# Latent attention: scores of a head as three products of high and low parts, with the queries scaled before they are transposed

## The reference, cut to what matters

```python
q = (rmsnorm(c_q, q_norm_g) @ w_q_up).reshape(B, S, N_HEADS, QK_DIM)
kv = (rmsnorm(c_kv, kv_norm_g) @ w_kv_up).reshape(B, S, N_HEADS, 2 * HEAD_DIM)
k = jnp.concatenate([k_nope, jnp.broadcast_to(k_rope[:, :, None, :], ...)], axis=-1)
q = rmsnorm(q, q_head_g)
k = rmsnorm(k, k_head_g)
q = jnp.concatenate([q[..., :HEAD_DIM], rope(q[..., HEAD_DIM:], positions)], axis=-1)
...
logits = jnp.einsum('bhqd,bhkd->bhqk', qi, k) * scale     # blocks of 128 queries
w = jax.nn.softmax(jnp.where(mask, logits, -jnp.inf), axis=-1)
o = jnp.einsum('bhqk,bhkd->bhqd', w, v)
o = o * jax.nn.silu(gate)
```

## Time and profile before

| | before |
|---|---|
| median of 3 runs | 1319.96 us |
| the profiled execution | 1320.29 us |
| its span in the trace | 1318.1 us |
| TensorE busy | 1297.5 us (98%) |
| VectorE busy | 762.6 us (58%) |
| ScalarE busy | 639.9 us (49%) |
| GpSimd busy | 344.7 us (26%) |
| mean granted TensorE clock | 0.999 |

### The profile page before, as it was taken

The page is one execution under the profiler, slowest core; times in us unless marked ns, Lnnn a source line. Parts: engine busy times, 40 slices in busy tenths (PEclk is TensorE's granted clock), DMA queues, the critical chain, the costliest instruction groups (busy, mean ns, idle before and its releaser), DMA issues.

```text
span 1318.1 us, 17841 instructions
## 1 busy us (share of the span) xinstructions
PE 1297.5 (98%) x6478; PEld 1086.4 (82%) x6478; DVE 762.6 (58%) x1205; ACT 639.9 (49%) x1159; POOL 344.7 (26%) x393
## 2 busy tenths in 40 slices
PE   7999999999999999999999999999999999999998
PEld 6997878778888888888888878888888888888986
DVE  5656999835652235898444642335466335578843
ACT  5379778624532325998244422514244234355632
POOL 2228877400000007773000000000000000668620
PEclk9999999999999999999999999999999999999999
DMA  5332100122222232001322333332232321421121
GB/s 186 85 112 65 45 25 14 49 95 97 96 96 96 96 96 81 17 0 32 108 99 85 93 95 96 96 96 64 85 100 92 126 99 55 129 64 49 34 64 64
DMA packets 70595, 104.66 MB, mean 79 GB/s; under 512 B 3460, under 2 KB 30840, under 8 KB 70392
## 3 DMA queue, kind: packets, MB, share of 16 engines
q1 hardware_dynamic: 69312, 99.44, 24.0%
q0 software_dynamic: 1088, 4.17, 1.1%
q10 hardware_dynamic: 120, 0.05, 0.0%
HBM read 101.55 MB, written 2.10 MB: 79 GB/s over the span
## 4 chain that ended last, share of the span: by engine, by line
PE 90%; DVE 5%; ACT 2%; issue 2%; DMA 0%; DVEq 0%; POOL 0%; SPq 0%; ACTq 0%; POOLq 0%
PE ps L491 24%; PE ps L493 24%; PE ps L492 24%; PE ps L688 2%; PE ps L991 2%; PE ps L846 2%; PE ps L701 1%; PE ps L935 1%; PE ps L836 1%; PE ps L715 1%; PE ps L667 1%; PE ps L837 1%; DVE sp L2052 1%; PE ps L716 1%; DVE sp_l L2057 1%
## 5 line engine op out<-in xcount | busy, mean ns | idle before, releaser
L1655 DVE TENSOR_TENSOR w_lo<-stage,w_hi 128x1024 fp32r<-128x1024 f32 (+4 forms) x189 | 225.1, 1191 | 421.7 <-ACT w_hi L1087 421.6
L1087 ACT ACTIVATE w_hi<-stage 128x1024 fp32r<-128x1024 f32 (+4 forms) x189 | 192.0, 1016 | 463.2 <-PE ps L493 462.0
L491 PE MATMUL ps<-a0h,w_hi 128*128 128x512 f32 x512 | 204.6, 400 | 0.8 <-DVE q_lo L2232 0.8
L493 PE MATMUL ps<-a0h,w_lo 128*128 128x512 f32 x512 | 200.0, 391 | 0.0
L492 PE MATMUL ps<-a0l,w_hi 128*128 128x512 f32 x512 | 199.5, 390 | 0.0
L2336 POOL TENSOR_TENSOR small<-small 128x16 f32<-128x16 f32 (+2 forms) x14 | 32.4, 2317 | 391.1 <-DVE small L1733 285.9
L491 PE MATMUL ps<-w_hi,a0h 128*128 128x512 f32 (+1 forms) x320 | 122.3, 382 | 0.1
L493 PE MATMUL ps<-w_hi,a0l 128*128 128x512 f32 (+1 forms) x320 | 119.9, 375 | 0.0
L492 PE MATMUL ps<-w_lo,a0h 128*128 128x512 f32 (+1 forms) x320 | 119.8, 374 | 0.0
L493 PEld LDWEIGHTS ps<-a0h,w_lo 128*128 128x128 f32 x512 | 96.1, 188 | 20.6
L491 PEld LDWEIGHTS ps<-a0h,w_hi 128*128 128x128 f32 x512 | 96.2, 188 | 20.1 <-issue 1.3
(11 more groups left out here) (324 smaller groups left out, 2841.9 us busy)
## 6 DMA issues: line engine op xcount, KB each, us to landing
stage<-in_a_w_in SPq DMA_DIRECT2D x48, 512.0 KB, 3.8
stage<-in_ple_w_gate SPq DMA_DIRECT2D x16, 512.0 KB, 3.3
stage<-in_w_kv_shared SPq DMA_DIRECT2D x16, 512.0 KB, 3.6
stage<-in_sb_w_in SPq DMA_DIRECT2D x16, 512.0 KB, 3.7
stage<-in_a_w_out SPq DMA_DIRECT2D x16, 512.0 KB, 3.3
stage<-in_b_w_in SPq DMA_DIRECT2D x16, 512.0 KB, 3.7
stage<-in_mla_w_in SPq DMA_DIRECT2D x8, 512.0 KB, 3.9
stage<-in_sb_w_out SPq DMA_DIRECT2D x8, 512.0 KB, 3.3
```

The lines of the kernel that those rows point to most:

```text
L491: pe.matmul(bank, wh, mh, start=start and not seeded, stop=False, skip_group_check=seeded)
L493: return pe.matmul(bank, wl, mh, start=False, stop=stop, skip_group_check=seeded)
L1087: act.activation(slab(w_hi[r % 2], L, nk, w), slab(stage[r % 4], L, nk, w), ACT.Copy).then_inc(S("hi_ready"), 1)
L1655: dve.tensor_tensor(slab(w_lo[r % 2], L, nk, w), slab(stage[r % 4], L, nk, w), slab(w_hi[r % 2], L, nk, w), ALU.subtract)\
```

## The change

Scores are computed from high and low parts of queries and keys, in three fp32r products instead of one in float32. For that the queries must be scaled before they are transposed, which GpSimd does with a multiplication over all 96 columns in place of the copy of 64; the gain of the queries is negated, so the scores come out negative, the mask has the other sign, and the row minimum is at once the bias of the exponential. `qT_h`, `qT_l`, `kT_h` and `kT_l` have one buffer each. ScalarE reads the high part out of bank 6, and VectorE, after it, the low part (`head_lo`); `qT_ok` and `kT_ok` are now set by VectorE. Of the four blocks of probabilities VectorE scales the two long ones, ScalarE the two short ones. TensorE runs three steps of the gate tile between the transposes of queries and of keys, and one behind them.

Apart from the attention: the first load comes in two halves; the wait in `out0` is moved behind three more steps; the negated sink of the window attention is gone, and some semaphores of the last norm have other names.

```diff
-        "causal": np.where(i[None, :] <= i[:, None], 0.0, BIG),
+        "causal": np.where(i[None, :] <= i[:, None], 0.0, -BIG),
...
-    qT = [put(f"qT{s}", [P, T], 10 + 2 * s) for s in range(2)]
-    kT = [put(f"kT{s}", [P, T], 14 + 2 * s) for s in range(2)]
+    qT_h, qT_l = (put(f"qT_{n}", [P, T], kb, F32R) for n, kb in (("h", 10), ("l", 12)))
+    kT_h, kT_l = (put(f"kT_{n}", [P, T], kb, F32R) for n, kb in (("h", 14), ("l", 16)))
...
+            if r == 0:
+                sp_.dma_start(stage[0][:, 0:nk, 0:w // 2], src[:, :, 0:w // 2]).then_inc(S("first_in"), 16)
+                sp_.dma_start(stage[0][:, 0:nk, w // 2:w], src[:, :, w // 2:w]).then_inc(loaded[0], 16)
+                return
...
-                if k % 2 == 0:
+                if r == 0 and k == 0:
+                    pe.wait_ge(S("first_lo"), 1)
+                elif k % 2 == 0:
...
                     if L.name == "out0" and k == 0 and n == 3:
+                        continue
+                    if L.name == "out0" and k == 1 and n == 3:
                         pe.wait_ge(S("src_ready"), source(first_item["x0"]))
+                        products(0, n)
+                    if L.name == "proj0" and g == k == 0 and n == 2:
+                        pe.wait_ge(S("lo_ready"), 1)
                     if L.name == "q_up" and g == k == 0 and n == 3:
...
-                pe.matmul(ps[b][:, c:c + n], qT[s][0:QK, j * P:(j + 1) * P], kT[s][0:QK, 0:n],
-                          start=j != 0, stop=False, skip_group_check=True)
+                to, rows = ps[b][:, c:c + n], slice(j * P, (j + 1) * P)
+                pe.matmul(to, qT_h[0:QK, rows], kT_h[0:QK, 0:n], start=j != 0, stop=False, skip_group_check=True)
+                pe.matmul(to, qT_h[0:QK, rows], kT_l[0:QK, 0:n], start=False, stop=False, skip_group_check=True)
+                pe.matmul(to, qT_l[0:QK, rows], kT_h[0:QK, 0:n], start=False, stop=False, skip_group_check=True)
                 pe.matmul(ps[b][:, c + j * P:c + n], ident_r[:, :], causal_r[:, :], start=False, stop=True, skip_group_check=True)\
                     .then_inc(S("s_done"), 1)
...
-                pe.wait_ge(S("p_ready"), MB * h + (n + 1))
+                if n < 2:
+                    pe.wait_ge(S("p_ready"), 2 * h + n + 1)
+                else:
+                    pe.wait_ge(S("p_act"), 2 * h + n - 1)
...
-                mla_gate_tile(lin["mla_gate1"], i, 7, 4 * s, 4 * s + 2)
+                mla_gate_tile(lin["mla_gate1"], i, 7, 4 * s, 4 * s + 3)
...
-                out_rows(0, 4 * s, 4 * s + 2, (0,), s == 1)
+                out_rows(0, 4 * s, 4 * s + 3 - s, (0,), s == 1)
...
-                mla_gate_tile(lin["mla_gate1"], i, 7, 4 * s + 2, 4 * s + 4)
+                mla_gate_tile(lin["mla_gate1"], i, 7, 4 * s + 3, 4 * s + 4)
...
-                out_rows(0, 2, 4, (0,), False)
+                out_rows(0, 3, 4, (0,), False)
...
-        def head_T(h, s, sem, to, g, ok, bank=6):
+        def head_hi(h, sem, to, g, bank=6):
+
+
             act.wait_ge(S(sem), h + 1)
-            if not (isinstance(h, int) and h < 2):
-                act.wait_ge(S("s_done"), MB * (h - 1))
-            act.activation(to[s][0:QK, :], ps[bank][0:QK, :], ACT.Identity, scale=gain(g, 0, QK)).then_inc(S(ok), 1)
+            if h:
+                act.wait_ge(S("s_done"), MB * h)
+            act.activation(to[0:QK, :], ps[bank][0:QK, :], ACT.Identity, scale=gain(g, 0, QK)).then_inc(S("qk_hi"), 1)
...
-                               scale=scale, accum_out=ssum[:, j:j + 1]).then_inc(S("exp_done"), 1)
+                               scale=-1.0, accum_out=ssum[:, j:j + 1]).then_inc(S("exp_done"), 1)
...
-            probs(h, s, (lambda: head_T(h + 1, 1 - s, "qT_done", qT, "q", "qT_ok")) if more else None)
+            probs(h, s, (lambda: head_hi(h + 1, "qT_done", qT_h, "q")) if more else None)
             if more:
-                head_T(h + 1, 1 - s, "kT_done", kT, "k", "kT_ok")
+                head_hi(h + 1, "kT_done", kT_h, "k")
+            act.wait_ge(S("rsum_ok"), h + 1)
+            for j in (1, 0):
+                at = slice(QRY_COL[j], QRY_COL[j] + (j + 1) * P)
+                act.activation(pr[:, at], pr[:, at], ACT.Identity, scale=rsum[:, j:j + 1]).then_inc(S("p_act"), 1)
...
-        dve.wait_ge(S("q_ss_ok"), 4)
-
-        def maxima(h):
-            def scaled(j, n):
-                link.wait(n)
-                scale = q_ss[:, h, j:j + 1] if isinstance(h, int) else q_ss[:, bass.ds(h, 1), j]
-                dve.scalar_tensor_tensor(nb[:, j:j + 1], mx[:, j:j + 1], -1.0, scale, ALU.mult, ALU.mult).then_inc(S("nb_done"), 1)
-
-            last = None
+        def minima(h):
+
+
             for r, j in enumerate(reversed(range(MB))):
                 b, c = QRY_BANK[j]
                 dve.wait_ge(S("s_done"), MB * h + (r + 1 if j > 1 else MB))
-                n = link.mark(dve.tensor_reduce(mx[:, j:j + 1], ps[b][:, c:c + (j + 1) * P], AX.X, ALU.max))
-                if last:
-                    scaled(*last)
-                last = (j, n)
-                if r == 0:
-                    scaled(*last)
-                    last = None
-            scaled(*last)
+                dve.tensor_reduce(nb[:, j:j + 1], ps[b][:, c:c + (j + 1) * P], AX.X, ALU.min).then_inc(S("nb_done"), 1)
 
         def normalize(h):
             dve.wait_ge(S("exp_done"), MB * h + MB)
-            link(dve.reciprocal(rsum, ssum))
-            for j in reversed(range(MB)):
+            if h:
+                dve.wait_ge(S("p_act"), 2 * h)
+            dve.reciprocal(rsum, ssum).then_inc(S("rsum_ok"), 1)
+            dve.wait_ge(S("rsum_ok"), h + 1)
+            for j in (3, 2):
                 at = slice(QRY_COL[j], QRY_COL[j] + (j + 1) * P)
                 dve.tensor_scalar(pr[:, at], pr[:, at], rsum[:, j:j + 1], None, ALU.mult).then_inc(S("p_ready"), 1)
 
-        def probs_T(h):
+        def head_lo(n, high, low, g, ok, bank=6):
+
+            dve.wait_ge(S("qk_hi"), n)
+            dve.scalar_tensor_tensor(low[0:QK, :], ps[bank][0:QK, :], gain(g, 0, QK), high[0:QK, :], ALU.mult, ALU.subtract)\
+               .then_inc(S(ok), 1)
+
+        def probs_T(h, between=None):
             if h:
                 dve.wait_ge(S("o_done"), h)
             for b, (c, n) in enumerate(((0, T), (T, 384), (896, 384))):
+                if b == 1 and between:
+                    between()
                 dve.wait_ge(S("pT_a"), 3 * h + (b + 1))
                 dve.tensor_tensor(prT_l[:, c:c + n], ps[3 + b][:, 0:n], prT_h[:, c:c + n], ALU.subtract).then_inc(S("pT_b"), 1)
...
         def mla_step(h):
             i, s = h // 2, h % 2
-            maxima(h)
+            minima(h)
+            more = h < HEADS - 1
+
+            def q_low():
+                head_lo(2 * h + 3, qT_h, qT_l, "q", "qT_ok")
+
             if h:
-                probs_T(h - 1)
+                probs_T(h - 1, q_low if more else None)
+            else:
+                q_low()
             if h == 1:
                 split_to(lin["mla_gate1"].load0 + 1)
             normalize(h)
+            if more:
+                head_lo(2 * h + 4, kT_h, kT_l, "k", "kT_ok")
             if h == 0:
                 head_sums(k_ss, 4 * HD, "k")(lin["kv_up"], G, MB - 1, None)
...
                 mla_sum(h - 1)
 
+        head_lo(1, qT_h, qT_l, "q", "qT_ok", 0)
+        head_lo(2, kT_h, kT_l, "k", "kT_ok", 1)
         for h in range(HEADS):
...
-            dve.scalar_tensor_tensor(nb_w[s], mx_w[s], -1.0, neg_sink[:, h:h + 1].to_broadcast([P, MB]), ALU.mult, ALU.min).then_inc(S("wnb_done"), 1)
+            dve.tensor_scalar(nb_w[s], mx_w[s], sink[:, h:h + 1], -1.0, ALU.max, ALU.mult).then_inc(S("wnb_done"), 1)
...
-            pool.tensor_copy(q_ring[s][:, :, 0:HD], q[:, :, 0:HD])
-            rotate(q_ring[s][:, :, HD:QK], q[:, :, HD:QK], 0, s, "qk_ring")
+            scale = q_ss[:, h, :].rearrange("p (m o) -> p m o", o=1)
+            link(pool.tensor_tensor(q_ring[s][:, :, :], q, scale.to_broadcast([P, MB, QK]), ALU.mult))
+            turned = q_ring[s][:, :, HD:QK]
+            pool.tensor_tensor(rope_b[s][:, :, 0:16], turned[:, :, 16:32], rope[:, 1, :, 0:16], ALU.mult)
+            link(pool.tensor_tensor(rope_b[s][:, :, 16:32], turned[:, :, 0:16], rope[:, 1, :, 16:32], ALU.mult))
+            link(pool.tensor_tensor(turned, turned, rope[:, 0, :, :], ALU.mult))
+            pool.tensor_tensor(turned, turned, rope_b[s][:, :, :], ALU.add).then_inc(S("qk_ring"), 1)
```

More of the change, by code:

```diff
@@ L291, in build @@
     q_ss, k_ss = little(HEADS, MB), little(HEADS, MB)
-    mx, nb, ssum, rsum, esink = little(MB), little(MB), little(MB), little(MB), little(MB)
-    nb_w, ssum_w, es_w = ([little(MB) for _ in range(2)] for _ in range(3))
-    neg_sink = little(HEADS)
+    nb, ssum, rsum, esink = little(MB), little(MB), little(MB), little(MB)
+    nb_w, ssum_w = ([little(MB) for _ in range(2)] for _ in range(2))
+    both_w = [little(MB, 2) for _ in range(2)]
     mx_w = [little(MB) for _ in range(2)]
@@ L616, in do @@
```

(34 more changed lines are left out.)

14 lines of the change are left out of this document (6 added, 8 removed).

## The result

The changed kernel takes 1345.88 us (median of 4 runs, 1343.03 to 1346.32) against 1319.86 for the kernel before, run beside it: a ratio of 1.019 (95% interval 1.0177 to 1.0202), or +26.0 us. The forecast was 1335.0 with a range of 1325 to 1342. The direction was right; the size was not, and the time lies outside the range.

A forecast was written before the change was run, and what follows sets the result against it. TensorE, busy 98% of the span, was taken to bound the kernel. Terms of 14.4 (heads 2 to 14), +1.8 (edges), -1.1 (`out0`) and -0.1 (start) gave +15.0, so 1335.0 us, range 1325 to 1342.

The forecast's parts named there:

- The mechanism: Latent attention: values wait for VectorE's low part of the keys, about 0.7 us in even heads, near 1.9 in odd.
- New scores: Each latent attention head: three products take 2.34 us instead of 2.56, a gain of 0.22.
- lower bound of 2.13: New scores' time in us if a product needs only its columns' share without change of weights.
- four rivals: Short scalings 1328 (0.18), faster 1315 (0.10), whole GpSimd operations 1341 (0.10), scores not cheaper 1338.5 (0.05).
- whole exclusions: Rival, odd heads: each scaling waits for a whole GpSimd operation, loss 2.8 per head, +21.4 in all, 1341; chance 0.10.
- the edges of the attention: First scores +1.5, head 0 -0.4, head 1 +1.6, last head -0.9: together +1.8 us, taken as ±1.5.
- Head 0: First latent attention head: no values, TensorE's work 7.2 us against 7.61 before, so -0.4.
- Head 1: Second latent attention head: weight split and head 0's sums delay VectorE, values 1.0 later than other heads' 0.57: +1.6 us.
- The terms per head: Heads 2 to 14: seven even at 0.57 us and six odd at 1.73, 14.4 together.
- The start: First products could begin earlier, but transposes wait for the input's loads: -0.1 us, bounds ±0.4.
- `out0`: TensorE's wait of 1.15 us there is covered by nine products: -1.1, bounds 0 and -1.15.
- the last head: Last latent attention head: values' wait of 1.57 us for VectorE falls without the negating steps, -0.9.

The follow-up runs named there:

- Float32 scores: Changed kernel with float32 scores, bank 6 read once, double buffers and gate products 6 and 6: 1315.87 us, ratio 0.9966 to the kernel before.
- the small edits alone: Kernel before with only first weights in halves, delayed out0 product, and window attention's and last norm's small changes: 1318.23 us against 1320.54, ratio 0.9984.
- zero products: Changed kernel with zero-tile products in TensorE's waits, 7 before head 0's scores, 4 or 8 behind key transposes: 1340.59 us, ratio 1.0155 to the kernel before.
- a change of order on VectorE alone: Changed kernel with the key's low part ahead of the two scalings in every head: 1332.76 us, ratio 1.0098 to the kernel before.
- its pause: Kernel before with two throw-away VectorE readings that TensorE waits for ahead of head 0's scores: 1322.32 us, ratio 1.0014.
- Behind 2.9 us: Kernel before with four throw-away VectorE readings ahead of head 0's scores instead of two: 1325.56 us, ratio 1.0044.

## Why the prediction was wrong

**The mechanism was right.** The values wait for the key's low part in 14 heads (the forecast's 15 counts one too many, since head 0 has no values and the last head no keys), by about 1.1 in even and 2.2 in odd ones, for a forecast 0.7 and 1.9. Float32 scores take all of that away, and the run is then below the one with the small edits alone: scaling on GpSimd, the minima and ScalarE's two scalings cost nothing in the heads. No run has three products without the second reading, so the two were not priced apart. New scores took 2.39 (194.27 to 196.66) for a forecast 2.34; its lower bound of 2.13 is not worked out there, and nothing hung on it. None of the four rivals came as a time; what is true of the one for whole exclusions stands below.

**The step that failed: the clock, which the sum put at nothing, in the edges of the attention first.** Head 0 was put at -0.4 because "TensorE's work is 7.2". That counts its work at full clock, right behind the new wait of 1.5 that the same paragraph puts in front of it. The clock fell there, and head 0 took 10.23. The zero products brought it to 7.10, so the work was as forecast, and 3.1 of the 10.23 were clock. The same omission costs 1.0 in head 1 (3.37 from the values to the next scores, 2.34 in other heads), 0.5 in head 2 and 1.5 in head 5. That is 6.1 by the rows; the zero products gave back 5.3, as they also put off head 0's scores by 0.5. It is half of the 11.0 between forecast and result. No term of the sum and no bound had a clock in it. With the clock full the changed kernel takes 1340.59, 5.6 above the forecast and inside the range; the omitted clock is what puts it outside.

**Head 1** was put at +1.6 and lost 4.1. Its values started 9.81 after the scores, not 8.0. 1.0 of the 4.1 is clock. The rest is VectorE's queue: the sum of head 0's keys and the first minima made the query's low part late, the key transposes waited 0.98 for it, and then came a weight split of 1.21, which the forecast did name.

**The terms per head** were right in kind and small in size. Even heads: 9.63 - 8.81 = 0.82 each for a forecast 0.57. The chain is longer than its readings: the low part takes 0.74, not 0.68, and 0.28 pass from its end to the first product of the values (191.65 to 191.93) where I had allowed 0.03 to 0.05. Head 1's key transposes did start 0.05 behind the low part that they waited for:

```profile
133.94 0.74 DVE L1955 SCALAR_TENSOR_TENSOR qT_l<-ps,gains,qT_h 96x512 fp32r<-96x512 f32 x1
134.73 0.64 PE L678 MATMUL ps<-cst,k_ring 128*96 128x128 f32 x4 [0.98 <-DVE qT_l L1955]
```

Why the values come later behind theirs no run shows. Odd heads: 10.71 - 8.81 = 1.90 for 1.73, and 2.2 in head 13. The two scalings took 1.83 as against the 1.95 forecast, but started 0.17 later. Over 13 heads these sizes make 17.5 for 14.4.

**Whole exclusions.** The rule of the Trainium skill, "SBUF — State Buffer", section "Who interferes with whom", put the odd heads' two scalings at 2.9 us at its worst. They took 1.83 beside GpSimd's 1.39 and 0.82 where GpSimd was idle. By shape, head 7 has

```profile
L1950 DVE TENSOR_SCALAR pr<-pr,small 128x384 f32<-128x384 f32 x1 | 1.4, 1424 | 0.0
...
L1950 DVE TENSOR_SCALAR pr<-pr,small 128x512 f32<-128x512 f32 x1 | 0.5, 487 | 0.0
```

```profile
200.12 1.39 POOL L2466 TENSOR_TENSOR tmp<-q_tok,sgm 64x512 f32<-64x512 f32 x1
```

The first scaling, begun ahead of GpSimd, took the 0.49 of head 6; the second took 1.42 for head 6's 0.42 and ended at 201.74, 0.23 behind GpSimd's operation. So the trace agrees with the rule in kind: the second scaling stood for the rest of that operation. What was wrong in the worst case is its price, since only one of the two scalings met an operation; in head 13 both did, and they took 2.15. The cost is about 1 us here, not 2.

**The start** was bounded at ±0.4 and gave -1.28. In the trace before, the transposes of the input start 0.35 behind the release by its loads (14.71 for 14.36), held by the twelve products in front of them. That the loads would hold them next was right; that these land at 14.36 was not fixed. The profile after, and below it the run with the small edits alone:

```profile
8.22 0.80 PE L495 MATMUL ps<-pTh,w_hi 128*128 128x512 f32 x1 [1.16 <-DVE w_lo L1685]
...
13.48 1.94 PE L636 MATMUL ps<-cst,x_tok 128*128 128x128 f32 x16
13.64 0.79 POOL L2383 DMA_DIRECT2D head_g<-in_mla_q_head_g  x1 [13.20 <-DMA x_tok<-in_x]
```

```profile
13.88 1.94 PE L637 MATMUL ps<-cst,x_tok 128*128 128x128 f32 x16 [0.95 <-DMA x_tok<-in_x]
14.04 0.79 POOL L2362 DMA_DIRECT2D head_g<-in_mla_q_head_g  x1 [13.60 <-DMA x_tok<-in_x]
```

TensorE's first twelve products began 1.75 earlier (8.22 for 9.97). In eight of the nine profiles with the first load in halves the transposes start 0.16 ahead of the GpSimd instruction that the same loads release, in six of them after a named wait on the loads of 0.45 to 0.95. That instruction starts between 13.64 and 14.19 in the nine, and between 13.96 and 14.45 in the four with one load, so the loads differ from one execution to the next; whether the halves bring them earlier was not separated. The transposes start at 13.48 to 14.07 for 14.11 to 14.71, and the pair before and after has the two ends, 1.23 apart. Some of the gain was lost again at 113, where the first query transposes now wait 0.85; the forecast had looked at GpSimd's longer program in the steady heads only.

**`out0`** and the last head came out as forecast (-2.03 for -2.0).

## What to carry to other kernels

A second reading of a shared PSUM bank puts its own length and a handover in front of the bank's next writer, unless the cover behind it is as long (0.8 us per even head here, with three products of cover). Look at what stands before that reading on its engine: here a change of order on VectorE alone gave back 13 of 26 us, 7.8 of them against the run at full clock and 5.3 by the clock. When a change puts idle time into a dense stretch of TensorE, price the clock too, and price it as a range: behind waits of 1.5 to 1.7 us the profiles showed from nothing to 3.1 us more, and behind most waits of 2.2 to 2.5 us nothing.

## What the runs showed that I had not expected

- Behind a wait of 1.66 us the clock stayed at 0.5 for 6.8 us in the changed kernel, for 3.4 us behind 1.6 in the kernel before with its pause, and not at all in the profiled execution with the key's low part first. Behind 2.9 us it fell in the profiled execution for 6.8 us, and all five times were high (1324.9 to 1326.5). The page "TensorE: Matmul & The Clock Gate" of the Trainium skill, section "Part 1: The HAM clock gate", describes such a gate with a half rate for an idle array; the two levels agree with the granted clock here.
- More work made the kernel faster: 7 zero products ahead of head 0 and 4 or 8 per head took 5.3 us off.
- From the end of VectorE's low part to TensorE's first product 0.25 to 0.28 us passed in front of the values of heads 2 to 14, about 0.15 in front of head 0's scores and head 1's values, and 0.05 in front of head 1's key transposes.
